# A two-layer hybrid encoder on one Trainium2 core: five units' low halves taken on VectorE instead of GpSimd beside the state-space scan

## What is computed

```python
proj = x @ w_in
(r_q, r_k, r_v, r_z, s_u, s_z, m_x, m_v, m_o, m_z, m_i, m_f, a_q, a_z) = split(proj)
ret = retention(r_q, r_k, r_v, positions) * silu(r_z)
s5o = s5(s_u, ...) * silu(s_z)          # complex diagonal state-space scan over the tokens, then a GLU
ml  = head_norm(mlstm(...)) * silu(m_z)
xa  = memory_attention(a_q, mem @ xa_w_kv) * silu(a_z)
y   = concatenate([ret, s5o, ml, xa]) @ w_out
x   = layer_norm(ALPHA * x + y)
```

## Time and profile before

| | us |
|---|---|
| median of 3 runs | 1873.7 (1871.24 to 1877.73) |
| the profiled execution, as timed | 1873.72 |
| its span in the trace | 1871.9 |
| PE busy | 1798.6 (96%) |
| weight loads busy | 1578.5 (84%) |
| DVE busy | 1035.0 (55%) |
| ACT busy | 604.4 (32%) |
| POOL busy | 522.4 (28%) |
| longest wait of PE in the list of waits, ended by DVE `wlo` L1638 at the program's start | 17.3 |

### The profile page before, as it was taken

The page is one execution under the profiler, slowest core; times in us unless marked ns, Lnnn a source line. Parts: engine busy times, 40 slices in busy tenths (PEclk is TensorE's granted clock), DMA queues, the critical chain, the costliest instruction groups (busy, mean ns, idle before and its releaser), DMA issues.

```text
span 1871.9 us, 27041 instructions
## 1 busy us (share of the span) xinstructions
PE 1798.6 (96%) x10992; PEld 1578.5 (84%) x10992; DVE 1035.0 (55%) x2002; ACT 604.4 (32%) x853; POOL 522.4 (28%) x238
## 2 busy tenths in 40 slices
PE   5999999999999999999989999999999999999997
PEld 5878897889988998878887788978999889988786
DVE  6997615461374378339649675254613825772524
ACT  4442344431124313432243332444311242143320
POOL 2443213112121413345336232121211131134451
PEclk9999999999999999999999999999999999999999
DMA  7435355132023205674335333541410331167451
GB/s 249 150 114 142 96 188 202 46 101 70 24 68 132 94 24 209 216 272 148 101 111 167 110 101 113 192 158 57 125 34 24 107 119 68 33 244 281 148 165 52
DMA packets 99187, 236.54 MB, mean 126 GB/s; under 512 B 10864, under 2 KB 41920, under 8 KB 97784
## 3 DMA queue, kind: packets, MB, share of 16 engines
q1 hardware_dynamic: 73064, 184.25, 30.4%
q10 hardware_dynamic: 25920, 50.34, 7.3%
q0 software_dynamic: 80, 0.23, 0.0%
HBM read 171.60 MB, written 58.98 MB: 123 GB/s over the span
## 4 chain that ended last, share of the span: by engine, by line
PE 79%; DVE 8%; DMA 6%; ACT 4%; issue 2%; POOL 2%; ACTq 0%; SPq 0%; DVEq 0%
PE gp L573 19%; PE gp L575 18%; PE gp L574 18%; DMA wraw<-in_w 4%; PE mm L573 2%; PE mm L575 2%; PE mm L574 2%; DMA yraw<-yt 2%; POOL wlo L1072 2%; PE mm L785 1%; PE mm L694 1%; ACT whi L1149 1%; DVE sz L1838 1%; PE mm L763 1%; PE mm L925 1%
## 5 line engine op out<-in xcount | busy, mean ns | idle before, releaser
L1072 POOL TENSOR_TENSOR wlo<-wraw,whi 128x1024 fp32r<-128x1024 f32 x168 | 434.9, 2606 | 1152.0 <-ACT whi L1149 1151.8
L573 PE MATMUL gp<-whi,xh 128*128 128x256 f32 x1280 | 382.0, 298 | 0.0
L575 PE MATMUL gp<-whi,xl 128*128 128x256 f32 x1280 | 362.8, 283 | 0.0
L574 PE MATMUL gp<-wlo,xh 128*128 128x256 f32 x1280 | 362.5, 283 | 0.0
L573 PE MATMUL gp<-xh,whi 128*128 128x512 f32 x768 | 321.5, 419 | 5.3 <-ACT xh L1190 2.9
L575 PE MATMUL gp<-xh,wlo 128*128 128x512 f32 x768 | 302.2, 394 | 0.0
L574 PE MATMUL gp<-xl,whi 128*128 128x512 f32 x768 | 301.6, 393 | 0.0
L573 PEld LDWEIGHTS gp<-whi,xh 128*128 128x128 f32 x1280 | 245.9, 192 | 7.7 <-issue 7.5
L574 PEld LDWEIGHTS gp<-wlo,xh 128*128 128x128 f32 x1280 | 245.9, 192 | 4.8 <-issue 4.7
L1149 ACT ACTIVATE whi<-wraw 128x1024 fp32r<-128x1024 f32 x172 | 175.8, 1054 | 225.8 <-DMA wraw<-in_w 114.8
L575 PEld LDWEIGHTS gp<-whi,xl 128*128 128x128 f32 x1280 | 245.3, 192 | 0.0
(11 more groups left out here) (326 smaller groups left out, 2996.9 us busy)
## 6 DMA issues: line engine op xcount, KB each, us to landing
wraw<-in_w SPq DMA_DIRECT2D x172, 512.0 KB, 4.2
spill<-gate ACTq DMA_DIRECT2D x32, 512.0 KB, 2.6
yraw<-yt SPq DMA_DIRECT2D x32, 512.0 KB, 5.9
xr<-in_x SPq DMA_DIRECT2D x16, 512.0 KB, 9.0
xs<-xr SPq DMA_DIRECT2D x16, 512.0 KB, 5.0
ud<-gate ACTq DMA_DIRECT2D x8, 512.0 KB, 3.0
uu<-ud SPq DMA_DIRECT2D x64, 64.0 KB, 3.4
p_tab<-kd SPq DMA_DIRECT2D x64, 64.0 KB
```

Of the source, the lines that this page charges most:

```text
L573: nc.tensor.matmul(out, ah, bh, start=start, stop=False)
L574: nc.tensor.matmul(out, ah, bl, start=False, stop=False)
L575: return nc.tensor.matmul(out, al, bh, start=False, stop=stop)
L1072: nc.gpsimd.tensor_tensor(wlo[slot(u)][:, 1024 * i:1024 * i + 1024], wraw[n % 2], whi[slot(u)][:, 1024 * i:1024 * i + 1024].bitcast(F32), ...
```

## The change

DVE takes the low halves of the units U_SZ+1, U_AQ, U_AQ+1, U_RZ and U_RZ+1 (7 to 11), two instructions each, in both layers. Each pair stands at a fixed place of DVE's program: behind the second scan of rounds 0, 3 and 5 for U_SZ+1, U_AQ+1 and U_RZ, and at the end of rounds 1 and 6 for U_AQ and U_RZ+1. POOL keeps U_SZ (unit 6) and all units from U_GL (12) on, and makes the rows of rounds 2 to 7 one after the other; it then waits until the halves before U_GL are counted. SP, ACT and PE have the same programs as before.

```diff
@@ POOL @@
                 rows(l, 0)
                 rows(l, 1)
                 lo(l, U_SZ)
-                rows(l, 2)
-                lo(l, U_SZ + 1)
-                rows(l, 3)
-                lo(l, U_AQ)
-                rows(l, 4)
-                rows(l, 5)
-                lo(l, U_AQ + 1)
-                rows(l, 6)
-                lo(l, U_RZ)
-                rows(l, 7)
-                for u in range(U_RZ + 1, U_LO + 1):
+                for q in range(2, NPB):
+                    rows(l, q)
+                pool.wait_ge(S["lo_done"], l * HALVES + half0(U_GL))
+                for u in range(U_GL, U_LO + 1):
                     lo(l, u)
@@ DVE @@
+            def window_lo(l, u):
+
+                for i in range(2):
+                    n = l * HALVES + half0(u) + i
+                    dve.wait_ge(S["lo_done"], n)
+                    dve.wait_ge(S["hi_done"], n + 1)
+                    TT(wlo[slot(u)][:, 1024 * i:1024 * i + 1024], wraw[n % 2],
+                       whi[slot(u)][:, 1024 * i:1024 * i + 1024].bitcast(F32), ALU.subtract).then_inc(S["lo_done"], 1)
+
@@ DVE @@
                 for q in range(NPB):
                     scan(l, 2 * q)
                     scan(l, 2 * q + 1)
+                    if q in (0, 3, 5):
+                        window_lo(l, {0: U_SZ + 1, 3: U_AQ + 1, 5: U_RZ}[q])
                     if q + 2 < NPB:
                         angles(l, q + 2)
                     if q + 1 < NPB:
                         end_tables(l, q + 1)
                     if q + 2 < NPB:
                         vectors(l, q + 2)
+                    if q in (1, 6):
+                        window_lo(l, U_AQ if q == 1 else U_RZ + 1)
```

## The result

The changed kernel takes 1883.19 us (median of 20 runs, 1875.23 to 1889.8), the kernel before 1872.22 us (median of 20, 1867.1 to 1878.01). The ratio is 1.0054 with a 95% interval of 1.0041 to 1.0067: it is slower by 8 to 13 us. The forecast was 1882.6 us with a range of 1877.5 to 1890.

A forecast was written before the change was run, and what follows sets the result against it. PE bounds the kernel (79% of the chain that ended last), waiting for `kd` loads queued on SP behind low halves. 10.8 + 3.4 - 4.9 - 0.4 = +8.9 us on 1873.72 gives 1882.6 us, range 1877.5 to 1890.

The forecast's parts named there:

- the link: State-space stage: a chain of low half, weight load, `kd` load and PE, whose first link is what is moved.
- the nameless wait at line 712: PE's waits without a releaser in rounds 2 and 5, 1.46 to 2.46 us, taken to be for the convolution table.
- Round 5: U_RZ's low halves end 5.4 us later on DVE, `kd` slides, PE stands 7.1 and 7.9 us: +10.8 us together.
- The backlog rival: Round 5: both raw loads stand right in front of `kd`, which lands 6.1 us after issue: +21, 1895 us; 8%.
- The clock: Behind the long waits of round 5 TensorE's clock falls to 0.51 for 3.5 us: +3.4 us for both layers.
- its dear bound of 2.5 us: Upper bound for the low clock behind round 5, about 2.5 us each, from matmul spacing after the program's start.
- Round 2: U_AQ's pair ends sooner on DVE, `kd_load(2)` goes out 1.8 us sooner: waits -3.2, low clock -1.7, together -4.9 us.
- Round 0 of layer 1: PE's 2.53 us wait for `zs` gains little, since `kd_load(0)` lands no sooner: -0.4 us, bounds 0 and 2.5.
- The sum: All terms over both layers: 10.8 + 3.4 - 4.9 - 0.4 = +8.9 us on 1873.72 us gives 1882.6 us.
- The rule on the shared port: VectorE two-input and GpSimd SBUF operations take turns on one port pair; by it alone only -4.9 and -0.4 us.

The follow-up runs named there:

- the first experiment: Changed kernel with `kd_load(5)` moved on SP ahead of the raw loads of U_RZ+1: 1862.5 us, ratio 0.9948 to the kernel before.
- the pair with the cut link: `kd_load(2)` and `kd_load(5)` ahead of the raw loads on SP: in the kernel before 1865.28 us, 0.9962; in the changed kernel 1863.54 us, 0.9956.
- the one with the delay in round 5: Changed kernel with U_RZ's first subtraction done twice more on DVE ahead of the pair, 2.44 us in each layer: 1890.01 us, ratio 1.0087.

## Why the prediction was right

**What bounds the kernel, and the link.** Right: the nameless wait at line 712 was for the `kd` loads, and these hung on U_RZ's low halves through SP's order. This had been read from the order of issues and the code; the first experiment shows it, since nothing but SP's order was touched.

**Round 5.** Forecast: waits of 7.1 and 7.9 us, +10.8 us together. Found: 7.38 and 7.29, which is +5.7 and +4.8, together +10.6. The halves' spacing, the two clean scans (5.5 us) and the 0.5 us from low half to `kd` issue all came as worked out. Issue to release was 5.7 and 5.6 us, between the two values of the same round (5.4 and 6.2). The backlog rival, for which the raw loads now stand closer before `kd`, wasn't seen.

**The clock.** Forecast +3.4. Found: 2.7 and 1.6 us by the granted clock, 2.5 and 1.5 us by the shifts, together +4.0; in layer 0 the low clock lasted longer than the 3.5 us that were taken over from round 2. The Trainium skill's rule ("TensorE: Matmul & The Clock Gate", what is actually happening) agrees for every wait over 7 us here: all six, in three kernels, have a granted clock of 0.50 to 0.55 behind them. It leaves open the waits of about 2 us, some of which cost a low clock and some not: behind 1.88 us (U_RZ ahead of scan 10, round 2 of layer 0) the granted clock was 0.69, behind 3.27 us (the kernel before with `kd` early, round 0 of layer 1) it was 1.00. The forecast also read too much from the first pair of matmuls. A pair of 0.77 us does show a low clock, but one of 0.46 or 0.49 us doesn't show a full one, since the clock can fall just behind it, as it does behind 1028.69 in the kernel before (below). And its dear bound of 2.5 us, from the program's start, isn't shown to be clock: the granted clock reads 1.00 from 17.2 to 23.0 us, where the matmuls are 0.21 us apart.

**Round 2.** Forecast -4.9. By the shifts it is -1.8 in layer 0 and -1.2 for the wait and -1.6 for the clock in layer 1, -4.5. For layer 0 that is partly luck. The wait was 0.53 us in the kernel that moves only U_RZ's pair and 1.88 in the one with U_RZ ahead of scan 10, so single traces don't show a gain there. In layer 1 they do: 2.02 and 2.22 us with U_AQ's pair on POOL, 0.84 and four times under 0.5 with it on DVE.

**Round 0 of layer 1.** Forecast -0.4. The wait itself is the same (2.53 and 2.62), since now the table ends it instead of `zs`: the bound from `kd_load(0)`'s issue was the right one. The low clock behind it didn't come this time. Before, it had cost 1.5 us by the shifts, which the forecast named in its bound but left out of its -0.4:

```profile
1028.60:1032.20 3.60, 3.51 (x17) 3.12 (x18) 3.46 (x10) 1.72 (x4) 0.00 (x0) 0.70 0.63 214
```

That the change took it away isn't shown: a low clock stands behind the same wait in the changed kernel with both `kd` loads early (0.68 from 1030.5 to 1034 us), and none in the kernel before with the same edit.

**The sum.** The terms as found are 10.6 + 4.0 - 4.5 - 1.5 and -0.2 at round 0 of layer 0, which is the 8.3 of the two stages within rounding; the ratio says 10.1. The forecast said 8.9. The mechanism and its largest term were right. The agreement to a microsecond is partly luck: a clock term too small and a round 0 term too small cancel, and 2.5 us of the traces' difference lie outside the stages.

**The rule on the shared port.** The prediction weighed the Trainium skill's rule ("SBUF — State Buffer", two separate sides), by which DVE would only gain. The row it put beside the rule is a copy, with one input; the rows of the operations that the rule names, with two inputs in SBUF, agree with it: `zc` and `zs` take 2.45 and 2.56 us beside POOL's pair and 0.42 us without. The relief is real: DVE took 24.4 us of work and is 0.6 us longer busy. Not every outlier went, as had been expected, since POOL keeps its rows: the scans of batch 0 in layer 1 take 2.58 us beside them (1030.78) where others take 0.75. The relief is worth nothing measurable where PE doesn't stand for DVE, as the pair with the cut link shows (0.9962 and 0.9956, each known to about 0.0015).

## What to carry to other kernels

A producer's place in its engine's program sets more than when its own result is there: through buffer reuse it times the next load, and through an in-order issue queue every unrelated transfer written behind that load. So before work is moved to a less loaded engine, follow its semaphore to each issuer that waits for it, and see what is queued there. Where a small urgent transfer stands behind a bulk load that waits for a buffer, reordering the issuer is the cheaper edit: it gave as much by itself (0.9962) as with the move to VectorE (0.9956).

## What the runs showed of the hardware that was not expected

Two traces of the same instructions can show waits of PE that differ by 1 to 2 us, for two reasons.

In round 0 of layer 0 it isn't the landing. The changed kernel, the one with U_RZ ahead of scan 10 and the one with the delay in round 5 run the same instructions up to there, and PE stood 1.43, 0.89 and 2.73 us. But from the first `kd` issue to PE's release it took 4.5 us in all three (107.62 to 112.10, 107.52 to 112.04, 107.54 to 112.05). What differed is when PE came. From 98 to 109 us the granted clock was 0.84 in the first two and 1.00 in the third, where PE came 1.3 and 1.8 us sooner and only stood longer. So a low clock ahead of a wait whose end is fixed by a load costs nothing, and a wait that grew need not mean a later load.

In round 2 of layer 0 the landing itself scatters. The first `kd` issue was at 142.43 us in the changed kernel and at 142.40 with U_RZ ahead of scan 10, and PE came at 150.7 and 150.8. In the one it didn't have to wait; in the other it was released 10.3 us after the issue:

```profile
152.69 0.46 PE L712 MATMUL mm<-uu,p_tab 128*128 128x128 f32 x2 [1.88 <-issue]
```

In the kernel that moves only U_RZ's pair it took 7.0 us (144.69 to 151.67). In round 5, over ten stretches in five kernels where PE waits, it took 5.2 to 6.3 us. So single traces carry a microsecond or two in a wait like that of round 2, and a low clock more or less behind it, which is why only the ratios over many runs decide between kernels that lie 2 us apart.
